# One transfer per expert in place of two, in a two-layer trunk with routed experts

## The chip, the cores and the metric

The kernel runs on one core of a Trainium2 chip. The metric is the device time of one execution in microseconds (us); the median of 3 runs is given. Everything is written in Bass: five instruction streams, one for each engine, that meet only at semaphores.

## What is computed

The reference is a decoder trunk of two layers over 256 tokens of width 1024, all in float32. Layer 0 mixes with a recurrent block, layer 1 with attention over shared keys and values. After its mixer each layer runs a mixture of experts, and that is the part in question:

```python
def moe_ffn(x, router_w, router_b, w_gate, w_up, w_down, s_gate, s_up, s_down):
    ...
    _, e_idx = lax.top_k(choice, TOPK_EXPERTS)          # 8 of 64 experts for each token
    ...
        hdn = jax.nn.silu(xs @ w_gate[e]) * (xs @ w_up[e])
        y = (hdn @ w_down[e]).astype(jnp.float32) * wt[:, None]
        return acc.at[tok].add(y), None
    ...
    shared = (jax.nn.silu(xt @ s_gate) * (xt @ s_up)) @ s_down
    return (acc.astype(x.dtype) + shared).reshape(B, S, D)
```

An expert has w_gate and w_up (1024 x 256 each) and w_down (256 x 1024): 3 x 1 MB of float32. All 64 experts of a layer are used, so each layer reads 192 MB of expert weights.

## The kernel before, in words

**Weights in SBUF.** The tile `weights` holds 18 units of 8 KB per partition. `E(s)` (L202) is expert slot s, three units wide, 24 KB per partition: the first 16 KB (`GU` = 4096 elements) hold gate and up, interleaved by contraction chunk, the last 8 KB hold down. There are four slots, in two pairs: slots 0 and 1 are pair 0, slots 2 and 3 pair 1. In HBM an expert lies in the same layout, 128 rows of 24 KB.

**The expert loop.** Both layers run the same loop, 16 iterations of two pairs (b = 0 and 1), so 64 experts. A pair is two blocks of up to 64 tokens, each in one half of the array's columns. For a pair TensorE does, in this order (L505 to L551): 16 gate/up matmuls 128x512; the scatter of the pair before, in two halves; for b = 1 also the gather of the next iteration's four blocks, by one-hot matmuls; the transposes of the hidden values and of the weighted one-hot; 8 down matmuls 128x512. ScalarE and VectorE evict, scale and split between these.

**What TensorE waits for.** Before a pair's gate/up matmuls it waits for `gu{b}_loaded` (L509), before the down matmuls for `down{b}_loaded` (L541). It counts up `gu_mm` when the gate/up matmuls of a pair are done (L517) and `down_mm` twice, once for each half of the down matmuls (L551).

**What orders the loads.** SyncE's queue issues all weight loads in program order. In `expert_loop` (L287) it reads the numbers of the pair's two experts from a table, waits until the gate/up matmuls of the same pair in the iteration before are done (L295), issues the two gate/up transfers of 2 MB (L297), waits until the down matmuls of that pair are done (L301), and issues the two down transfers of 1 MB (L303). The loop runs for iterations 1 to 15; the experts of iteration 0 are loaded ahead of it by `expert` (L258), again in two transfers each. Transfers of one queue start in the order of issue.

```python
                        sp.wait_ge(S(f"gu_mm_{L}"), i * 2 + (b - 1))
                        ...
                        sp.wait_ge(S(f"down_mm_{L}"), i * 4 + (2 * b - 2))
```

Of the kernel before, what the change touches and what calls it, by code (L numbers as in the profile page):

```python
# [65 lines left out]
EXPERT = 3 * UNIT  # L66
GU = KC * 2 * DE
# [12 lines left out]
def build(nc, xt_d, x_d, pt_d, cst_d, cstb_d, chan_d, rows_d, tab_d, win_d, gates_d, wout_d, shared_d,  # L80
          router_d, experts_d, ple_d, pgate_d, wkv_d, wq_d, wo_d, out_d):
    ctx = ExitStack()
    with ctx:
# [3 lines left out]
        def sem(name):  # L87
            return ctx.enter_context(nc.semaphore(name))
# [100 lines left out]
        def S(name):  # L189
            if name not in names:  # L190
                names[name] = sem(name)
            return names[name]
# [9 lines left out]
        def E(s):  # L202
            return W[:, 3 * s:3 * s + 3, :].rearrange("p a n -> p (a n)")
# [29 lines left out]
        def unit(name):  # L233
            return W[:, loaded_at[name][0], :]
# [18 lines left out]
        @block.sync  # L253
        def _(sp):
            def load(name, src):
                sp.dma_start(unit(name), src).then_inc(unit_sem[loaded_at[name][0]], 16)

            def expert(L, s, e):  # L258
                sp.dma_start(E(s)[:, 0:GU], experts_d[L, e, :, 0:GU]).then_inc(S(f"gu{s // 2}_loaded_{L}"), 16)
                sp.dma_start(E(s)[:, GU:EXPERT], experts_d[L, e, :, GU:EXPERT]).then_inc(S(f"down{s // 2}_loaded_{L}"), 16)  # L260

            sp.dma_start(chan[:, :], chan_d).then_inc(small, 16)
            sp.dma_start(xT[:, :, :], xt_d).then_inc(xt_in, 16)
            for i in range(4):
                load(f"win{i}", win_d[i])
            sp.dma_start(cst[:, :], cst_d).then_inc(small, 16)
            sp.dma_start(bconst[:, :, :], cstb_d).then_inc(small, 16)
            load("gates0", gates_d[0])
            load("gates1", gates_d[1])
            for i in range(4, 8):  # L270
                load(f"win{i}", win_d[i])
            for i in range(4):
                load(f"wout{i}", wout_d[i])
            load("sh0_0", shared_d[0, 0])
            load("sh1_0", shared_d[0, 1])
            sp.wait_ge(S("xb_mm"), KC)
            expert(0, 0, 0)
            sp.wait_ge(S("gate_mm"), KC)
            expert(0, 1, 1)
            for i, u in enumerate(("sh2_0", "pg0_0", "pg1_0", "pg2_0")):  # L280
                sp.wait_ge(S("yb_mm"), 2 * i + 2)
                load(u, shared_d[0, 2] if i == 0 else pgate_d[0, i - 1])
            sp.wait_ge(S("mix_mm"), TC * 2)
            expert(0, 2, 2)
            expert(0, 3, 3)

            def expert_loop(L):  # L287
                sp.wait_ge(S("table"), 1 * L + 1)
                n = sp.value_load(tab[0:1, L, 0, TABLE - 1:TABLE], min_val=NITER_MIN, max_val=NITER_MAX)
                with sp.Fori(1, n) as i:  # L290
                    for b in range(2):
                        es = [sp.value_load(tab[0:1, L, 1, bass.ds(i * 4 + 2 * b + s, 1)], min_val=0, max_val=NE - 1)
                              for s in range(2)]

                        sp.wait_ge(S(f"gu_mm_{L}"), i * 2 + (b - 1))  # L295
                        for s in range(2):
                            sp.dma_start(E(2 * b + s)[:, 0:GU],  # L297
                                         experts_d[L, bass.ds(es[s], 1), :, 0:GU].rearrange("a p n -> (a p) n")
                                         ).then_inc(S(f"gu{b}_loaded_{L}"), 16)

                        sp.wait_ge(S(f"down_mm_{L}"), i * 4 + (2 * b - 2))  # L301
                        for s in range(2):
                            sp.dma_start(E(2 * b + s)[:, GU:EXPERT],  # L303
                                         experts_d[L, bass.ds(es[s], 1), :, GU:EXPERT].rearrange("a p n -> (a p) n")
                                         ).then_inc(S(f"down{b}_loaded_{L}"), 16)
                last = sp.value_load(tab[0:1, L, 0, TABLE - 2:TABLE - 1], min_val=NITER_MIN - 1, max_val=NITER_MAX - 1)
                return n, last

            sp.wait_ge(S("shared_gu_mm"), TC)
            load("pg3_0", pgate_d[0, 3])  # L310
            load("ple_0", ple_d[0])
            sp.wait_ge(S("shared_down_mm"), 1)
            load("wk0", wkv_d[0, 0])
            n, last = expert_loop(0)
            sp.wait_ge(S("down_mm_0"), last * 4 + 2)
            for i in range(1, 4):
                load(f"wk{i}", wkv_d[0, i])
            for i in range(3):
                load(f"wv{i}", wkv_d[1, i])
            sp.wait_ge(S("down_mm_0"), n * 4)  # L320
            load("wv3", wkv_d[1, 3])
            for i in range(4):
                load(f"wq{i}", wq_d[i])
            load("wo0", wo_d[0])
            sp.wait_ge(S("pgate_mm"), TC * 2)
            for i in range(1, 4):
                load(f"wo{i}", wo_d[i])
            load("sh0_1", shared_d[1, 0])
            load("sh1_1", shared_d[1, 1])
            sp.wait_ge(S("k_mm"), TC * 2)  # L330
            load("sh2_1", shared_d[1, 2])
            expert(1, 0, 0)
            sp.wait_ge(S("v_mm"), TC * 2)
            expert(1, 1, 1)
            sp.wait_ge(S("q_mm"), TC * 2)
            expert(1, 2, 2)
            sp.wait_ge(S("mix_mm"), 4 + TC * 2)
            expert(1, 3, 3)
            for i in range(3):
                load(f"pg{i}_1", pgate_d[1, i])  # L340
            sp.wait_ge(S("shared_gu_mm"), 2 + TC)
            load("pg3_1", pgate_d[1, 3])
            load("ple_1", ple_d[1])
            expert_loop(1)
            for c in range(TC):
                for h in range(2):
                    sp.wait_ge(S("x_out"), 4 + 2 * c + h + 1)
                    sp.dma_start(out_d[0, P * c:P * c + P, HALF * h:HALF * h + HALF],
                                 x_res[:, c, HALF * h:HALF * h + HALF]).then_inc(out_s, 16)
            sp.wait_ge(out_s, 16 * TC * 2)  # L350
# [3 lines left out]
        def _(pe):  # L354
# [76 lines left out]
            def moe(L):  # L431
# [72 lines left out]
                n = pe.value_load(tab[0:1, L, 0, TABLE - 1:TABLE], min_val=NITER_MIN, max_val=NITER_MAX)  # L504
                with pe.Fori(0, n) as i:  # L505
                    for b in range(2):
                        g = i * 2 + b

                        pe.wait_ge(S(f"gu{b}_loaded_{L}"), i * 32 + 32)  # L509
                        if b == 0:  # L510
                            pe.wait_ge(S(f"gathered_{L}"), i * 4 + 4)
                        pe.wait_ge(S(f"hidden_{L}"), g + 1)
# [25 lines left out]
                            m = nc.tensor.transpose(PS[:, 7, (2 + c) * P:(3 + c) * P], ohw[:, c, :], ident)  # L538
                        m.then_inc(S(f"turn_mm_{L}"), 1)

                        pe.wait_ge(S(f"down{b}_loaded_{L}"), i * 32 + 32)  # L541
                        pe.wait_ge(S(f"hidT_{L}"), g + 1)
                        if b == 1:
                            pe.wait_ge(S(f"gathered_{L}"), i * 4 + 8)
# [12 lines left out]
            def ple(L):  # L557
# [16 lines left out]
                for t in range(TC * 2):  # L574
# [4 lines left out]
                    m.then_inc(S("pgate_mm"), 1)  # L579

            moe(0)
            ple(0)

# [89 lines left out]
            for c in range(TC):  # L673
                for h in range(2):
                    for k in range(KC):
                        m = mm(bank(2 * c + h), oT[:, k, c * P:c * P + P],
                               kmajor(f"wo{k // 2}")[:, k % 2, h * HALF:h * HALF + HALF], k == 0, k == KC - 1)
                    m.then_inc(S("mix_mm"), 1)
            moe(1)
            ple(1)  # L680

# [609 lines left out]
```

## Time and profile before

| | |
|---|---|
| runs | 1463.49, 1464.17, 1466.36 us; median 1464.17 us |
| profiled execution | 1463.85 us, its span 1462.0 us |
| TensorE busy | 1354.2 us, 93% of the span, 6158 matmuls |
| VectorE, ScalarE, GpSimd busy | 466.7, 291.7, 14.6 us |
| DMA | 460.65 MB, mean 315 GB/s |
| granted TensorE clock, mean | 0.973 |
| expert transfers | 128 of 2048 KB (median 11.1 us from issue to landing), 128 of 1024 KB (8.9 us) |

The span is what the engines take from the first to the last instruction; the execution's own time is 1.85 us longer. A stretch from about 188.5 to 654 us is the expert loop of layer 0, one from about 936.9 to 1406 us that of layer 1. Matmuls are pipelined, so that two of them overlap in the profile and a busy TensorE is not one at its peak. The times below are from the start of the span.

### The profile page before, as it was taken

To read this page: it belongs to the slowest core of one execution; us is meant where nothing else is said; L and a number is where in the kernel's file an instruction comes from. 1 tells how busy PE (TensorE), PEld (TensorE's weight loads), DVE (VectorE), ACT (ScalarE), POOL (GpSimd) and SP (SyncE) were. 2 spreads that over 40 slices of the span, in tenths; PEclk is the share of its full clock that TensorE was granted. 3 is DMA by queue.
4 is the path that set the end of the run, shared out by engine and by line. 5 is a ranking of instruction groups with operands and counts; after the bars stand their busy time and mean duration, and the time that the engine had idled before them with its cause. 6 is when DMAs were issued, how large, how long until landed. Compare 5 with 4: busy or idle time off the path is not lost.

```text
span 1462.0 us, 18637 instructions
## 1 busy us (share of the span) xinstructions
PE 1354.2 (93%) x6158; PEld 687.3 (47%) x6158; DVE 466.7 (32%) x1328; ACT 291.7 (20%) x502; POOL 14.6 (1%) x18
## 2 busy tenths in 40 slices
PE   6976799999999999998799687899999999999988
PEld 5843344544445444543444434454445444454443
DVE  3453433233332333234201324223332333323342
ACT  1502011221112111222201311121112211121121
POOL 0001000000000000000000001000000000000000
PEclk9988999999999999999799897999999999999999
DMA  9924289999999999985322214399999999999900
GB/s 377 387 106 172 87 366 423 423 422 416 417 419 426 420 419 421 422 343 237 144 115 87 87 55 189 153 425 417 414 420 420 420 419 412 419 421 420 404 29 29
DMA packets 46103, 460.65 MB, mean 315 GB/s; under 512 B 5249, under 2 KB 5506, under 8 KB 6658
## 3 DMA queue, kind: packets, MB, share of 16 engines
q1 hardware_dynamic: 44640, 453.48, 74.8%
q10 hardware_dynamic: 1442, 6.88, 1.2%
q8 instruction: 13, 0.21, 0.1%
q14 instruction: 8, 0.07, 0.0%
HBM read 459.30 MB, written 1.05 MB: 315 GB/s over the span
## 4 chain that ended last, share of the span: by engine, by line
PE 81%; DVE 9%; DVEq 4%; ACT 3%; issue 2%; DMA 1%; SPq 0%; ACTq 0%
PE ps L356 77%; DVEq L1095 3%; PE ps L533 1%; DVE onehot L1084 1%; PE ps L538 1%; DVE scratch L931 1%; DVE scratch L1108 1%; ACT y_hi L686 1%; DVE stats L946 1%; DMA weights<-in_win 1%; DVE x_res L963 1%; DVE x_res L968 1%; ACT z L686 1%; ACT scratch L686 1%; PE ps L427 1%
## 5 line engine op out<-in xcount | busy, mean ns | idle before, releaser
L356 PE MATMUL ps<-weights,scratch 128*64 128x512 f32 (+1 forms) x3232 | 749.1, 596 | 11.0 <-DVE scratch L1074 6.9
L356 PEld LDWEIGHTS ps<-weights,scratch 128*64 128x64 f32 (+1 forms) x3232 | 247.2, 140 | 464.2 <-issue 453.9
L686 ACT ACTIVATE scratch<-ps 128x512 f32<-128x512 f32 (+3 forms) x222 | 116.6, 526 | 585.5 <-PE ps L356 578.6
L1124 DVE SCALAR_TENSOR_TENSOR y_lo<-ps,slot_weight,y_hi 128x512 fp32r<-128x512 f32 x128 | 96.1, 750 | 179.8 <-ACT y_hi L686 179.8
L686 ACT ACTIVATE y_hi<-ps,slot_weight 128x512 fp32r<-128x512 f32 x128 | 88.0, 687 | 287.0 <-PE ps L356 287.0
L356 PE MATMUL ps<-weights,xT 128*128 128x512 f32 x320 | 138.5, 593 | 4.5 <-DVE xT L992 3.7
L356 PE MATMUL ps<-onehot,x_hi 128*128 128x256 f32 x544 | 113.5, 290 | 6.1 <-DVE onehot L1084 6.1
L356 PE MATMUL ps<-onehot,x_lo 128*128 128x256 f32 x544 | 110.1, 284 | 0.0
L356 PEld LDWEIGHTS ps<-onehot,x_hi 128*128 128x128 f32 x544 | 86.8, 192 | 35.1 <-issue 32.3
L356 PEld LDWEIGHTS ps<-weights,xT 128*128 128x128 f32 x320 | 60.3, 190 | 78.7 <-issue 74.6
L356 PE MATMUL ps<-y_hi,onehot_T 128*128 128x512 f32 x264 | 91.4, 427 | 3.3 <-DVE y_lo L1124 3.3
L356 PEld LDWEIGHTS ps<-onehot,x_lo 128*128 128x128 f32 x544 | 85.2, 192 | 0.0
L1108 DVE TENSOR_SCALAR scratch<-cst,rankt,wgtt 128x64 f32<-128x64 f32 x256 | 63.0, 309 | 64.4 <-issue 64.3
L356 PE MATMUL ps<-y_lo,onehot_T 128*128 128x512 f32 x264 | 82.7, 394 | 0.0
L1084 DVE TENSOR_SCALAR onehot<-cst,rankt 128x64 fp32r<-128x64 f32 x272 | 49.8, 279 | 88.7 <-issue 78.5
L1116 DVE COPY scratch<-ps 128x256 f32<-128x256 f32 x64 | 27.2, 425 | 155.1 <-PE ps L533 155.1
L1113 DVE TENSOR_TENSOR scratch<-scratch,ps 128x256 f32<-128x256 f32 x64 | 26.7, 417 | 137.3 <-ACT scratch L686 137.3
L356 PE MATMUL ps<-xT,weights 128*128 128x256 f32 x256 | 57.6, 388 | 11.9 <-DMA weights<-in_win 11.9
L356 PEld LDWEIGHTS ps<-xT,weights 128*128 128x128 f32 x256 | 49.8, 195 | 19.0 <-issue 11.9
L356 PEld LDWEIGHTS ps<-y_lo,onehot_T 128*128 128x128 f32 x264 | 49.5, 188 | 11.4
L356 PEld LDWEIGHTS ps<-y_hi,onehot_T 128*128 128x128 f32 x264 | 40.2, 190 | 31.2 <-issue 31.0
L1118 DVE TENSOR_REDUCE slot_weight<-ps 128x1 f32<-128x256 f32 x64 | 27.2, 424 | 46.2 <-PE ps L538 46.2
(139 smaller groups left out, 578.1 us busy)
## 6 DMA issues: line engine op xcount, KB each, us to landing
weights<-in_experts SPq DMA_DIRECT2D x128, 2048.0 KB, 11.1
weights<-in_experts SPq DMA_DIRECT2D x128, 1024.0 KB, 8.9
weights<-in_win SPq DMA_DIRECT2D x8, 1024.0 KB, 20.7
weights<-in_pgate SPq DMA_DIRECT2D x8, 1024.0 KB, 6.0
weights<-in_wkv SPq DMA_DIRECT2D x8, 1024.0 KB, 8.0
weights<-in_shared SPq DMA_DIRECT2D x6, 1024.0 KB, 11.8
weights<-in_wout SPq DMA_DIRECT2D x4, 1024.0 KB, 24.9
lnp<-in_rows ACTq DMA_DIRECT2D x4, 1024.0 KB, 5.3
```

The costliest lines, as they stand in the source:

```text
L356: return nc.tensor.matmul(out, lhsT, rhs, start=first, stop=last, skip_group_check=shared_bank)
L427: m = nc.tensor.transpose(PS[:, 4 + q, (2 * kk + c) * P:(2 * kk + c + 1) * P], src[:, c, k * P:k * P + P], ident)
L533: m = nc.tensor.transpose(PS[:, 6, f * P:f * P + P], hh[:, f * P:f * P + P], ident)
L538: m = nc.tensor.transpose(PS[:, 7, (2 + c) * P:(3 + c) * P], ohw[:, c, :], ident)
L686: return nc.scalar.activation(out, in_, f, **kw)
L1084: ins = v.tensor_scalar(oh[:, c, s * CAP:s * CAP + CAP], iota, rankt[:, c, bass.ds(cols[s], 1)], None, ALU.is_equal)
L1095: return dve.value_load(tab[0:1, L, 0, bass.ds(at, 1)], min_val=0, max_val=NOBLK)
L1108: ins = v.tensor_scalar(ohw[:, c, s * CAP:s * CAP + CAP], iota, rankt[:, c, bass.ds(cols[s], 1)], wgtt[:, c, bass.ds(cols[s], 1)], ALU.is_ ...
L1113: v.tensor_tensor(hh, sg, PS[:, 6, DE:2 * DE], ALU.mult).then_inc(S(f"hidden_{L}"), 1)
L1116: v.tensor_copy(hT.rearrange("p f s -> p (f s)"), PS[:, 6, 0:DE]).then_inc(S(f"hidT_{L}"), 1)
L1118: v.tensor_reduce(wslot[:, 0:1], PS[:, 7, DE:DE + T], AX_X, ALU.max)
L1124: v.scalar_tensor_tensor(y_lo[:, hs], PS[:, 4 + h, :], wslot[:, 0:1], y_hi[:, hs].bitcast(F32), ALU.mult, ALU.subtract).then_inc(S(f"y_out ...
```

## The change

```diff
             def expert(L, s, e):
-                sp.dma_start(E(s)[:, 0:GU], experts_d[L, e, :, 0:GU]).then_inc(S(f"gu{s // 2}_loaded_{L}"), 16)
-                sp.dma_start(E(s)[:, GU:EXPERT], experts_d[L, e, :, GU:EXPERT]).then_inc(S(f"down{s // 2}_loaded_{L}"), 16)
+                sp.dma_start(E(s), experts_d[L, e]).then_inc(S(f"pair{s // 2}_loaded_{L}"), 16)
...
-                        sp.wait_ge(S(f"gu_mm_{L}"), i * 2 + (b - 1))
-                        for s in range(2):
-                            sp.dma_start(E(2 * b + s)[:, 0:GU],
-                                         experts_d[L, bass.ds(es[s], 1), :, 0:GU].rearrange("a p n -> (a p) n")
-                                         ).then_inc(S(f"gu{b}_loaded_{L}"), 16)
-
                         sp.wait_ge(S(f"down_mm_{L}"), i * 4 + (2 * b - 2))
                         for s in range(2):
-                            sp.dma_start(E(2 * b + s)[:, GU:EXPERT],
-                                         experts_d[L, bass.ds(es[s], 1), :, GU:EXPERT].rearrange("a p n -> (a p) n")
-                                         ).then_inc(S(f"down{b}_loaded_{L}"), 16)
+                            sp.dma_start(E(2 * b + s), experts_d[L, bass.ds(es[s], 1)].rearrange("a p n -> (a p) n")
+                                         ).then_inc(S(f"pair{b}_loaded_{L}"), 16)
...
-                        pe.wait_ge(S(f"gu{b}_loaded_{L}"), i * 32 + 32)
+                        pe.wait_ge(S(f"pair{b}_loaded_{L}"), i * 32 + 32)
...
-                        pe.wait_ge(S(f"down{b}_loaded_{L}"), i * 32 + 32)
```

An expert comes in one transfer of 3 MB, 24 KB per partition. Both transfers of a pair are issued when the pair's down matmuls of the iteration before are done; the wait on the gate/up matmuls is gone. TensorE waits for the whole pair ahead of the gate/up matmuls and for nothing loaded ahead of the down matmuls.

On SyncE, in the body of the expert loop of layer 0, this stands for pair 0 before (L297 are the gate/up transfers, 128x4096; L303 the down transfers, 128x2048):

```order
L295 ISA
L297 ISA [waits gu_mm_0]
L297 DMA weights<-in_experts 128x4096
L297 ISA
L297 DMA weights<-in_experts 128x4096
L301 REGISTER_ALU
L303 ISA [waits down_mm_0]
L303 DMA weights<-in_experts 128x2048
L303 ISA
L303 DMA weights<-in_experts 128x2048
```

and this in the changed kernel:

```order
L294 REGISTER_ALU
L296 ISA [waits down_mm_0]
L296 DMA weights<-in_experts 128x6144
L296 ISA
L296 DMA weights<-in_experts 128x6144
```

The gate/up part has moved behind the wait on the down matmuls and is one transfer with the down part.

On TensorE, around the change from pair 0 to pair 1 in the same loop, this stands before (98 and 99 of its list are the down matmuls of pair 0, then come the gate/up matmuls of pair 1):

```order
L538 MATMUL ps<-cst,scratch 128x128 [waits weighted_0]
L538 MATMUL ps<-cst,scratch 128x128
L356 MATMUL ps<-weights,scratch 64x512 [waits hidT_0,down0_loaded_0]
L356 MATMUL ps<-weights,scratch 64x512 x7
L356 MATMUL ps<-weights,scratch 64x512 [waits hidden_0,gu1_loaded_0]
L356 MATMUL ps<-weights,scratch 64x512 x15
```

and this in the changed kernel (its L348 is L356 of before):

```order
L530 MATMUL ps<-cst,scratch 128x128 [waits weighted_0]
L530 MATMUL ps<-cst,scratch 128x128
L348 MATMUL ps<-weights,scratch 64x512 [waits hidT_0]
L348 MATMUL ps<-weights,scratch 64x512 x7
L348 MATMUL ps<-weights,scratch 64x512 [waits hidden_0,pair1_loaded_0]
L348 MATMUL ps<-weights,scratch 64x512 x15
```

No matmul has moved; the wait for the down part is gone, and the wait ahead of the gate/up matmuls now stands for both parts.

## Rows read from the trace of the kernel before

**Rows 1.** The page: busy time by engine, and the chain that ended last.

```profile
PE 1354.2 (93%) x6158; PEld 687.3 (47%) x6158; DVE 466.7 (32%) x1328; ACT 291.7 (20%) x502; POOL 14.6 (1%) x18
...
PE 81%; DVE 9%; DVEq 4%; ACT 3%; issue 2%; DMA 1%; SPq 0%; ACTq 0%
```

**Rows 2.** Busy time of both expert loops; last: clock, DMA share, GB/s.

```profile
188.50:654.00 465.50, 465.40 (x2373) 222.92 (x2372) 146.11 (x430) 92.81 (x157) 0.00 (x0) 1.00 0.99 415
936.90:1406.00 469.10, 466.46 (x2378) 223.63 (x2377) 146.53 (x431) 92.80 (x157) 0.00 (x0) 1.00 0.96 402
```

**Rows 3.** Waits of SyncE's queue: us in total, times, longest.

```profile
SPq L303 <- PE ps L356: 421.6, 60, 8.9
SPq L297 <- PE ps L356: 278.8, 60, 14.1
```

**Rows 4.** Timeline of SyncE, one iteration of layer 0 (start, us, what).

```profile
431.72 0.85 SPq L303 DMA_DIRECT2D weights<-in_experts  x2
438.62 0.96 SPq L297 DMA_DIRECT2D weights<-in_experts  x2
448.48 0.85 SPq L303 DMA_DIRECT2D weights<-in_experts  x2
455.33 0.86 SPq L297 DMA_DIRECT2D weights<-in_experts  x2
461.62 0.85 SPq L303 DMA_DIRECT2D weights<-in_experts  x2
```

**Rows 5.** Timeline of SyncE, first iteration of layer 1.

```profile
941.82 0.85 SPq L303 DMA_DIRECT2D weights<-in_experts  x2
...
958.58 0.85 SPq L303 DMA_DIRECT2D weights<-in_experts  x2
...
971.98 0.85 SPq L303 DMA_DIRECT2D weights<-in_experts  x2
```

**Rows 6.** DMA issues: the transfers issued at 455.33, 455.86, 461.62, us to landing.

```profile
weights<-in_experts SPq DMA_DIRECT2D x1, 2048.0 KB, 9.7
...
weights<-in_experts SPq DMA_DIRECT2D x1, 2048.0 KB, 14.1
...
weights<-in_experts SPq DMA_DIRECT2D x1, 1024.0 KB, 10.4
```

**Rows 7.** SyncE's issues of experts 2 and 3 of layer 0.

```profile
122.67 0.33 SPq L259 DMA_DIRECT2D weights<-in_experts  x1
...
124.00 0.62 SPq L260 DMA_DIRECT2D weights<-in_experts  x1
```

**Rows 8.** DMA issues: landing of the last, issued at 124.00 us.

```profile
weights<-in_experts SPq DMA_DIRECT2D x1, 1024.0 KB, 16.3
```

**Rows 9.** SyncE at 935.72 us, and the landings of the two transfers.

```profile
935.72 0.88 SPq L297 DMA_DIRECT2D weights<-in_experts  x2
...
weights<-in_experts SPq DMA_DIRECT2D x1, 2048.0 KB, 7.5
...
weights<-in_experts SPq DMA_DIRECT2D x1, 2048.0 KB, 11.8
```

**Rows 10.** SyncE at 186.19 us, and the landing of the second transfer.

```profile
186.19 0.87 SPq L297 DMA_DIRECT2D weights<-in_experts  x2
...
weights<-in_experts SPq DMA_DIRECT2D x1, 2048.0 KB, 12.8
```

**Rows 11.** TensorE timeline; in brackets its idle time before.

```profile
143.41 13.90 PE L356 MATMUL ps<-weights,xT 128*128 128x512 f32 x32
...
162.11 8.83 PE L356 MATMUL ps<-weights,scratch 128*128 128x512 f32 x16 [3.43 <-DVE scratch L1074]
...
174.09 0.48 PE L356 MATMUL ps<-onehot,x_hi 128*128 128x256 f32 x2 [3.00 <-DVE onehot L1084]
...
910.16 8.66 PE L356 MATMUL ps<-weights,scratch 128*128 128x512 f32 x16 [3.44 <-DVE scratch L1074]
```

**Rows 12.** TensorE by microsecond: busy (matmuls), granted clock, DMA.

```profile
162.00:163.00 1.00, 0.89 (x2) 0.67 1.01 418
163.00:164.00 1.00, 1.00 (x3) 0.50 0.94 385
...
166.00:167.00 1.00, 1.00 (x4) 1.00 0.00 0
...
172.00:173.00 1.00, 0.00 (x0) 1.00 0.46 115
...
174.00:175.00 1.00, 0.92 (x8) 1.00 1.00 426
```

## The prediction

> **What bounds the kernel now.** I read the page first: TensorE is busy for 93% of the span and is 81% of the chain that ended last [rows 1]. Then busy time by stage. In the expert loops TensorE has next to no idle time, 0.1 us in 465.5 and 2.6 us in 469.1, at full clock, and the DMA engines are busy for 0.99 and 0.96 of the same stretches at 415 and 402 GB/s [rows 2]. Two resources are full at once. Which of them paces? The queue that issues the loads answers it: SyncE always waits for TensorE, 421.6 us ahead of the down transfers and 278.8 us ahead of the gate/up transfers, 60 times each [rows 3], so 2 layers x 15 iterations x 2 pairs. TensorE paces the loop, and the loads keep up with little to spare. Whatever makes them later shows.
>
> The issue times give the period. The down matmuls of the pairs end at 431.72, 448.48 and 461.62 [rows 4]: pair 1 takes 16.76 us from the end of pair 0, pair 0 takes 13.14 us from the end of pair 1, the period is 29.90 us. In layer 1 the same ends are 941.82, 958.58 and 971.98 [rows 5]: 16.76 and 13.40 us.
>
> **The change, part by part.** An iteration must bring 4 x 3.146 MB = 12.58 MB, before and after. What moves is the time of issue. Before, the gate/up part of pair 1 (4.19 MB of 6.29) was issued at 438.62 and TensorE wanted it at 461.62, 23.0 us later. Now all of it is issued at 448.48, with 13.14 us to go.
>
> How long does a pair take to land? No row shows two transfers of 3 MB, so I bound it. The nearest is the first load of experts 2 and 3, 6.29 MB in four transfers into an idle queue: issued from 122.67, the last one issued at 124.00 and landed 16.3 us later, at 140.30 [rows 7, 8], which is 17.6 us. From the start of layer 1's loop, 4.19 MB issued at 935.72 landed at 943.2 and, the second transfer being issued 0.55 us after the first, at 948.1 [rows 9]: 12.4 us for both, and 4.85 us for each further 2.10 MB (432 GB/s), so 17.2 us for three times 2.10 MB. The same at the start of layer 0's loop: 186.73 + 12.8 = 199.5, which is 13.3 us after the issue [rows 10], plus 4.85 is 18.2, the high end. For the low end: the same bytes in four transfers took 17.6 and in three would take 17.2, so two might save another 0.4: 16.8. I take 17.2, from rows 9, since there the loop's own instructions start on an idle queue. With 0.1 for the hand-over (my choice, small beside the bounds), TensorE can start a pair 17.3 us after the issue.
>
> *Pair 1 waits.* Its loads are issued at the end of its down matmuls; pair 0 then needs 13.14 us (layer 0) or 13.40 (layer 1). The rest is idle time of TensorE: 17.3 - 13.14 = 4.16 us and 17.3 - 13.40 = 3.90 us, in each of 15 iterations. 15 x (4.16 + 3.90) = 120.9 us. Nothing hides it: the scatter and the gather that could fill it stand behind the gate/up matmuls in TensorE's program, and in the loop before TensorE had no idle time that could swallow it [rows 2].
>
> *Pair 0 does not.* Its loads are issued when its own down matmuls end; before it is needed again pair 1 waits 4.1 us and works 16.76, so 20.9 us. Its data queue behind the tail of pair 1's. Transfers of the queue land in order: those issued at 455.33 and 455.86 landed at 465.0 and 470.0, the next, issued at 461.62, at 472.0 [rows 4, 6]. Behind the earlier pair, which lands 4.1 us after this issue, pair 0 lands 14.6 us later (three times 4.85), at 18.7: 2.2 us in hand. And the queue is idle when pair 1's loads are issued, so that these start as in rows 9. Only in the first looped iteration, with no stall ahead, does pair 0 wait 17.3 - 16.8 = 0.5 us, once in each layer: 1.0 us.
>
> *The clock.* A TensorE that idles for 4 us each period may lose its clock. Two idle stretches of 3.43 and 3.44 us stand in the trace; the same number of matmuls after them took 8.83 and 8.66 us where half of 13.90 is 6.95 [rows 11], a loss of 1.9 and 1.7. The granted clock was at 0.50 in 163:164, from the first microsecond after the gap, and back at 1.00 by 166; after the 3.00 us without a matmul ahead of 174.09 [rows 11] it stayed at 1.00 [rows 12]. Stalls of 3.9 to 4.2 us are longer than all three. A longer gap lets part of the half-clock time fall into the gap itself, where it costs nothing, so I take 1.5 us for each stall, with ends of 1.0 and 1.9 (the low one a guess, were half the time to fall into the gap): 30 x 1.5 = 45 us. It falls into pair 1, which is TensorE's work throughout, so it lengthens the period in full.
>
> *What is removed.* 120 issues and two waits per pair on SyncE, one wait on TensorE: nothing waited for them, as SyncE sat waiting for TensorE before each [rows 3]. In the loads ahead of the loop, experts 2 and 3 of layer 0 landed at 140.3, before the shared expert's matmuls even start [rows 8, 11]; merged or not, they are early. Zero. The loads behind the loop are issued relative to its end and shift with it. Zero.
>
> **The sum.** 1463.85 (the profiled execution's own time, 0.3 below the median of the runs) + 120.9 + 1.0 + 45 = 1630.8 us; against the median 1631.1. I predict 1631.
>
> One formula would come out lower. The Trainium skill, "DMA: Bandwidth & Descriptors", section "Anatomy of one DMA", gives a fixed 2.0 us plus the bytes over 436 GB/s for a DMA; an estimate from that page for a pair is 2.0 + 14.4 = 16.4 us, stalls of 3.4 and 3.1 us, and 1606 us in all. It was fitted on another way of issuing, and rows 7 to 9 measure the thing itself on this queue, so they decide.
>
> **The rivals.**
>
> *The clock stays up.* For: the gap of 3.0 us left it up. Against: both gaps of 3.4 us did not, and these are longer. Without the 45 us: 1586. If only some of the stalls cost it, between 1586 and 1631.
>
> *The loads of the two pairs share the engines.* Pair 0's loads are issued about 4 us before pair 1's have landed, with some 3 us of data left. If they took turns, pair 1 would land 3 us later: 30 x 3 = 90 more, 1721. Against: landings in order, 2 us apart for the next 1.05 MB [rows 6].
>
> *Faster.* The loop could be paced by its DMAs, not by TensorE: they are 0.99 busy at only 415 GB/s, while two transfers in a row land at 432. If long rows of 24 KB brought that rate throughout, 12.58 MB would take 29.1 us in place of 29.9, 30 x 0.8 = 24 us less: 1440. It decides only if a pair lands within 13.14 us of its issue, else the stall comes first; with no fixed cost at all that is 479 GB/s. Against: 432 measured, and TensorE's waits show no DMA in the loop. The Trainium skill speaks for this side too: "DMA: Bandwidth & Descriptors", section "Rules for kernel authors", advises to coalesce many small transfers into one large and to move at least 1 MiB at a time; by it alone the change could only help. No row here shows a transfer below 1 MB that is held back.
>
> *No difference.* If TensorE's program let the stall be filled, nothing would be lost; the order of its instructions rules this out, and there is no spare time in the loop either [rows 2].
>
> **How the numbers follow.** My forecast has 0.86 (the stall of pair 1 with the clock loss), the clock that stays up 0.07, sharing loads 0.05, faster 0.01, no difference 0.01. A measurement of this kernel tells about 0.2% (3 us) from no change. The forecast's own bounds are 16.8 us and 1.0 us: 1463.85 + 15 x (3.76 + 3.50) + 30 + 0.2 = 1603; and 18.2 and 1.9: 1463.85 + 15 x (5.16 + 4.90) + 57 + 3 = 1675. Both at their worst together is unlikely, so the top is 1660; the bottom reaches down to 1595, toward the case in which only some stalls cost the clock. Slower by over 0.2% is 0.98.
>
> **What would show it.** Right: TensorE's waits of 3.7 to 4.5 us at the gate/up matmuls, released by the load of weights, in pair 1 only, 30 of them, some 121 us in total; a period of 35.6 us in the loop (17.3 + 16.8 + 1.5); a granted clock of 0.50 for a few microseconds in each period; DMA idle for several microseconds in each period, landings of 16 to 18 us for the second transfer of a pair. The stages outside the loops keep their lengths. Wrong: stalls ahead of pair 0 as well, or stalls of 7 us (sharing); a clock of 1.00 throughout (1586); a period of 30 us.

## The result, and the profile after

| | before | changed |
|---|---|---|
| median | 1465.04 us (4 runs, 1463.49 to 1466.36) | 1681.35 us (4 runs, 1679.03 to 1683.09) |
| ratio | | 1.1476 (95% interval 1.1454 to 1.1497) |
| profiled execution, its span | 1463.85, 1462.0 us | 1683.09, 1681.2 us |
| mean granted TensorE clock | 0.973 | 0.919 |

The change costs 15%. The direction and the place were as predicted, the size was not: 216 us where 166 were forecast, and 1681 lies outside the range (1595 to 1660).

The page of the changed kernel, against [rows 1]:

```profile
PE 1444.2 (86%) x6158; PEld 703.5 (42%) x6158; DVE 467.0 (28%) x1328; ACT 291.5 (17%) x502; POOL 14.5 (1%) x18
...
PE 59%; DMA 31%; DVE 6%; ACT 2%; issue 1%; SPq 1%; DVEq 0%; ACTq 0%
PE ps L348 57%; DMA weights<-in_experts 30%; SPq L296 1%; DVE scratch L922 1%; DVE stats L937 1%; DMA weights<-in_win 1%; DVE x_res L954 1%; DVE x_res L959 1%; ACT z L677 1%; PE ps L419 1%; ACT scratch L677 1%; DVE z L964 0%; PE ps L525 0%; PE ps L530 0%; PE ps L641 0%
```

The loads of experts were nowhere in the chain that ended last; now they are 30% of it. VectorE, ScalarE and GpSimd do the same work in the same time. TensorE runs the same 6158 matmuls and is busy 90 us longer. (The counts are records of the trace; the expert matmuls have two each, so that a pair's 16 gate/up matmuls stand as x32.)

The waits of the changed kernel (us in total, times, longest):

```profile
PE ps L348 <- DMA weights<-in_experts: 131.3, 32, 4.8
```

and the expert matmuls, grouped by form, of the kernel before and, second, of the changed one (busy us, mean ns of one | idle before):

```profile
L356 PE MATMUL ps<-weights,scratch 128*64 128x512 f32 x3072 | 673.8, 594 | 1.5 <-ACT scratch L686 1.5
```

```profile
L348 PE MATMUL ps<-weights,scratch 128*64 128x512 f32 x3072 | 760.8, 652 | 132.8 <-DMA weights<-in_experts 131.3 <-ACT scratch L677 1.5
```

Two numbers hold the whole result: 131.3 us of idle time that a load ends, and 760.8 - 673.8 = 87.0 us more for the same matmuls, 218.3 together; the profiled executions differ by 219.2. The 32 waits are 15 ahead of pair 1 in each layer and one ahead of pair 0 in each layer's first looped iteration. Of the 30 ahead of pair 1, 29 are followed by slow gate/up matmuls. TensorE's timeline around three of them (start, us, what, idle time before):

```profile
228.32 8.78 PE L348 MATMUL ps<-weights,scratch 128*64 128x512 f32 x32 [3.29 <-DMA weights<-in_experts]
...
452.04 10.00 PE L348 MATMUL ps<-weights,scratch 128*64 128x512 f32 x32 [4.55 <-DMA weights<-in_experts]
...
1090.79 7.09 PE L348 MATMUL ps<-weights,scratch 128*64 128x512 f32 x32 [2.78 <-DMA weights<-in_experts]
```

At full clock they take 7.09 us. After 2.78 us of idle time they still do, after 3.29 they lose 1.7, after 4.55 they lose 2.9. Of the 30 stalls of pair 1, 26 are of the last kind (2.5 to 3.0 us lost). By microsecond around the middle one (after the length: TensorE busy, then weight loads, VectorE, ScalarE and GpSimd; the last three columns are granted clock, DMA share, GB/s):

```profile
450.00:451.00 1.00, 0.00 (x0) 0.00 (x0) 0.79 (x4) 0.00 (x0) 0.00 (x0) 1.00 0.97 418
451.00:452.00 1.00, 0.00 (x0) 0.00 (x0) 0.00 (x0) 0.00 (x0) 0.00 (x0) 0.56 0.97 418
452.00:453.00 1.00, 0.96 (x4) 0.35 (x6) 0.00 (x0) 0.00 (x0) 0.00 (x0) 0.50 1.03 442
...
457.00:458.00 1.00, 1.00 (x4) 0.24 (x2) 0.00 (x0) 0.00 (x0) 0.00 (x0) 0.53 1.20 516
458.00:459.00 1.00, 1.00 (x8) 0.41 (x6) 0.00 (x0) 0.00 (x0) 0.00 (x0) 1.00 1.03 442
```

The clock falls to half at about 451.1, 0.9 us ahead of the first matmul, and is back at about 457.9: 6.8 us at half, of which 5.9 are worked. The length of the gap alone does not set this. After a stall of 4.20 us in layer 1 the clock fell only at about 1386.4, 1.0 us into the matmuls (columns: TensorE busy, clock, DMA share, GB/s):

```profile
1385.36 8.78 PE L348 MATMUL ps<-weights,scratch 128*64 128x512 f32 x32 [4.20 <-DMA weights<-in_experts]
```

```profile
1385.00:1386.00 1.00, 0.64 (x4) 1.00 0.91 393
1386.00:1387.00 1.00, 1.00 (x5) 0.69 1.03 442
...
1389.00:1390.00 1.00, 1.00 (x4) 0.61 0.97 418
```

There it was at half for 3.4 us, all of them worked, and 1.7 us were lost. In the 26 stalls that cost 2.5 us or more it fell 0.7 to 1.7 us ahead of the first matmul and stayed at half for 6.8 us.

The chain of waits shows one stall from end to end:

```profile
430.74 3.61 PE ps L348 x16
434.35 0.02 issue
...
434.51 0.33 SPq L296
...
435.04 16.96 DMA weights<-in_experts
451.99 0.04 issue
452.04 14.94 PE ps L348 x68
```

Down matmuls, issue, 17.0 us of loading, next matmuls. From the first issue at 434.51 to the landing at 451.99 are 17.5 us, against 13.14 us of other work. The period is 37.6 us (434.51 to 472.11) where it was 29.90 [rows 4].

### The profile page after: what moved, and what is told of

It is laid out like the page before. It is cut to its first block, busy times and chain, and to the rows that moved or that the text cites. A ratio compares the mean times of both kernels' runs of the same rounds, so it can differ in the third digit from the quotient of the medians.

```text
span 1681.2 us, 18175 instructions
## 1 busy us (share of the span) xinstructions
PE 1444.2 (86%) x6158; PEld 703.5 (42%) x6158; DVE 467.0 (28%) x1328; ACT 291.5 (17%) x502; POOL 14.5 (1%) x18
## 4 chain that ended last, share of the span: by engine, by line
PE 59%; DMA 31%; DVE 6%; ACT 2%; issue 1%; SPq 1%; DVEq 0%; ACTq 0%
PE ps L348 57%; DMA weights<-in_experts 30%; SPq L296 1%; DVE scratch L922 1%; DVE stats L937 1%; DMA weights<-in_win 1%; DVE x_res L954 1%; DVE x_res L959 1%; ACT z L677 1%; PE ps L419 1%; ACT scratch L677 1%; DVE z L964 0%; PE ps L525 0%; PE ps L530 0%; PE ps L641 0%
## 5 line engine op out<-in xcount | busy, mean ns | idle before, releaser
L348 PE MATMUL ps<-weights,scratch 128*64 128x512 f32 (+1 forms) x3232 | 836.3, 651 | 142.3 <-DMA weights<-in_experts 131.3
L348 PEld LDWEIGHTS ps<-weights,scratch 128*64 128x64 f32 (+1 forms) x3232 | 261.9, 152 | 668.0 <-issue 503.0
L348 PE MATMUL ps<-weights,xT 128*128 128x512 f32 x320 | 138.5, 593 | 4.5 <-DVE xT L983 3.7
L348 PE MATMUL ps<-onehot,x_hi 128*128 128x256 f32 x544 | 113.5, 291 | 6.0 <-DVE onehot L1075 6.0
L348 PE MATMUL ps<-onehot,x_lo 128*128 128x256 f32 x544 | 110.1, 284 | 0.0
L348 PEld LDWEIGHTS ps<-onehot,x_hi 128*128 128x128 f32 x544 | 86.7, 192 | 34.9 <-issue 32.2
L348 PE MATMUL ps<-y_hi,onehot_T 128*128 128x512 f32 x264 | 91.5, 428 | 3.3 <-DVE y_lo L1115 3.3
L348 PEld LDWEIGHTS ps<-weights,xT 128*128 128x128 f32 x320 | 60.4, 190 | 78.6 <-issue 74.5
L348 PEld LDWEIGHTS ps<-onehot,x_lo 128*128 128x128 f32 x544 | 85.3, 193 | 0.0
L348 PE MATMUL ps<-y_lo,onehot_T 128*128 128x512 f32 x264 | 82.6, 394 | 0.0
L348 PE MATMUL ps<-xT,weights 128*128 128x256 f32 x256 | 58.6, 392 | 12.0 <-DMA weights<-in_win 12.0
L348 PEld LDWEIGHTS ps<-xT,weights 128*128 128x128 f32 x256 | 50.5, 198 | 19.3 <-issue 12.0
L348 PEld LDWEIGHTS ps<-y_lo,onehot_T 128*128 128x128 f32 x264 | 49.6, 188 | 11.4
L348 PEld LDWEIGHTS ps<-y_hi,onehot_T 128*128 128x128 f32 x264 | 40.2, 190 | 31.2 <-issue 31.0
```

What stands on the lines that cost most here:

```text
L348: return nc.tensor.matmul(out, lhsT, rhs, start=first, stop=last, skip_group_check=shared_bank)
```

## The experiments

Each was timed beside the kernel before on the same chip.

**1. The late issue alone.** The kernel before with all four transfers and both waits, but everything issued behind the wait on the down matmuls:

```diff
-                        sp.wait_ge(S(f"gu_mm_{L}"), i * 2 + (b - 1))
+                        sp.wait_ge(S(f"down_mm_{L}"), i * 4 + (2 * b - 2))
                         for s in range(2):
                             sp.dma_start(E(2 * b + s)[:, 0:GU],
...
-                        sp.wait_ge(S(f"down_mm_{L}"), i * 4 + (2 * b - 2))
                         for s in range(2):
                             sp.dma_start(E(2 * b + s)[:, GU:EXPERT],
...
```

> The kernel before with its four transfers and its two waits, but all four issued when the pair's down matmuls are done: the late issue alone, without the merging. Theory A (the loss comes from TensorE having to wait for all 6.29 MB ahead of the gate/up matmuls): the gate/up part, 4.19 MB, lands some 12.4 us after the issue, and TensorE has 13.14 to 13.40 us, so there is no stall or one of under 0.5 us, and the clock stays up: 1464 to 1475 us. Rival B (the late issue by itself starves the loop, since the DMA engines were full before): 1600 us or more.

Measured: 1464.96 us, ratio 0.9997 (0.9986 to 1.0007), 11 runs. TensorE's waits for experts:

```profile
  PEld ps L355: 12.2, 30
  PE ps L355: 0.2, 1
```

No stall but one of 0.2 us. The weight loads wait 0.4 us each, which the array hides. So the late issue by itself costs nothing, although the gate/up parts are issued 6.3 us (pair 0) and 9.9 us (pair 1) later than in [rows 4]. Theory A held, rival B fell.

**2. One wait, four transfers.** The changed kernel with each expert cut into 2 MB and 1 MB again, both on the pair's semaphore:

```diff
-                            sp.dma_start(E(2 * b + s), experts_d[L, bass.ds(es[s], 1)].rearrange("a p n -> (a p) n")
+                            sp.dma_start(E(2 * b + s)[:, 0:GU],
+                                         experts_d[L, bass.ds(es[s], 1), :, 0:GU].rearrange("a p n -> (a p) n")
+                                         ).then_inc(S(f"pair{b}_loaded_{L}"), 16)
+                            sp.dma_start(E(2 * b + s)[:, GU:EXPERT],
+                                         experts_d[L, bass.ds(es[s], 1), :, GU:EXPERT].rearrange("a p n -> (a p) n")
                                          ).then_inc(S(f"pair{b}_loaded_{L}"), 16)
...
-                        pe.wait_ge(S(f"pair{b}_loaded_{L}"), i * 32 + 32)
+                        pe.wait_ge(S(f"pair{b}_loaded_{L}"), i * 64 + 64)
```

> The changed kernel with each expert's transfer cut into two again (2 MB and 1 MB, one behind the other), both counted by the same semaphore: late issue and one wait for the pair, without the merging. Theory A: the merging itself neither costs nor gains; the pair lands within 0.4 us of the changed kernel's, 1678 to 1695 us. Rival B (rows of 24 KB make the transfer slow): back toward 1600 us, stalls below 4 us.

Measured: 1676.93 us, ratio 1.1454 (1.1436 to 1.1471). Its expert matmuls:

```profile
L353 PE MATMUL ps<-weights,scratch 128*64 128x512 f32 x3072 | 756.6, 649 | 130.1 <-DMA weights<-in_experts 128.5 <-ACT scratch L682 1.5
```

128.5 us of stalls and 82.8 us of slow matmuls, against 131.3 and 87.0. The time is 1 us below the expected range. The transfer of 3 MB is no better than its two parts; the 4.4 us by which it is slower are hardly clear of the noise (the intervals of the ratios overlap), and 2.4 of the 2.8 us between the stalls are one stall, the first of pair 1 in layer 1 (0.41 us in place of 2.78). Theory A held: given the late issue, the merging costs only because the gate/up matmuls then wait for the down weights too.

Run 1 shows that the late issue without the merged wait is free. The merged wait without the late issue was not run. In the kernel before the last down transfer of pair 1 is this one (SyncE's timeline; us to landing):

```profile
449.00 0.33 SPq L303 DMA_DIRECT2D weights<-in_experts  x1
...
weights<-in_experts SPq DMA_DIRECT2D x1, 1024.0 KB, 11.1
```

It landed at 460.1, and pair 1's gate/up matmuls began at about 461.4. An estimate from these rows is that a merged wait with the early issue would have found both parts there. The loss then takes both halves of the change, and one transfer for each expert brings both, since the buffer of its down part comes free last.

**3. Keeping the array busy through the stall.** The changed kernel with n matmuls of unused result ahead of pair 1's wait; bank 6 is free there:

```diff
+                        if b == 1:
+                            for _ in range(n):
+                                mm(PS[:, 6, :], ident, x_res[:, 0, 0:HALF], True, True, True)
                         pe.wait_ge(S(f"pair{b}_loaded_{L}"), i * 32 + 32)
```

With n = 10:

> The changed kernel with ten matmuls of 128x512 whose result is not used, ahead of pair 1's wait for its load: some 4.3 us of work in the stall. Theory A (of the loss, 131 us are stalls and 87 us are gate/up matmuls at half clock, 2.9 us each): the clock stays at 1.00, the stall stays as it is, and the 87 us go: 1683 - 87 = 1596, plus some 4 us in each of the two first iterations that have no stall, so 1598 to 1612 us. Rival B (the longer gate/up matmuls come from reading weights while the DMA engines write others, not from the clock): no gain, 1683 us or more.

Measured: 1751.06 us, ratio 1.1958 (1.1940 to 1.1976), so neither number. I had taken 0.43 us for one full-width matmul, which is what one of a pair on column halves takes (7.09 us for 16). Its rows (x640 are 320 matmuls):

```profile
L348 PE MATMUL ps<-weights,scratch 128*64 128x512 f32 x3072 | 680.8, 595 | 1.5 <-ACT scratch L680 1.5
L348 PE MATMUL ps<-x_res,cst 128*128 128x512 f32 x640 | 283.2, 597 | 0.0
```

Ten take 8.85 us (283.2 / 32), twice the stall; no wait for a load is left, and the expert matmuls are back at 680.8 us. The clock theory had that part right; the time needed the right n. So n = 5, 3, 2 and 1:

> The changed kernel with five of the matmuls of unused result ahead of pair 1's wait, not ten: one takes 0.88 us (8.85 us for ten in the run before), so ten were 4.4 us longer than the stall that they should fill, and five, 4.4 us, fill it. Theory A (the gate/up matmuls after a stall are slow by the clock alone): the clock stays at 1.00 in the loop, the gate/up matmuls take 7.1 us again in place of 10.0, the 87 us go, and the two first iterations, which have no stall, pay 4.4 us each: 1681 - 87 + 9 = 1603, 1598 to 1610 us. Rival B (they are slow by contention with the loads): 1681 us or more.

> The same with three: 2.6 us of work and 1.7 us idle in each stall. Theory A (the clock is lost by idle time of over 3 us, not by any): clock at 1.00, 1681 - 87 + 5 = 1599 us. Rival B (any gap costs a part in proportion to its length): about 1632 us.

> The same with two: 1.8 us of work and 2.6 us idle. Theory A: as with three, 1597 to 1600 us, since a gap of 3.0 us left the clock alone in the kernel before. Rival B (in proportion): about 1648 us.

> The same with one: 0.9 us of work and 3.5 us idle, as long as the gaps of the kernel before that cost 1.7 and 1.9 us. Theory A with my price of before (1.5 to 1.9 us a stall): 1681 - 87 + 2 + 30 x 1.7 = 1647 us, clock at half for some 3.3 us after each. If the price of the changed kernel holds for this gap too (2.9 us, half clock for over 6 us): 1683 us.

| n | idle before gate/up, in total | expert matmuls busy | mean clock | time |
|---|---|---|---|---|
| 0 (changed kernel) | 131.3 us | 760.8 us | 0.919 | 1681.35 us |
| 1 | 101.0 | 763.3 | 0.918 | 1686.96, ratio 1.1522 (1.1499 to 1.1545) |
| 2 | 75.4 | 698.0 | 0.968 | 1622.47, ratio 1.1082 (1.1055 to 1.1108) |
| 3 | 48.9 | 684.2 | 0.983 | 1607.64, ratio 1.0980 (1.0956 to 1.1005) |
| 5 | 0.6 | 680.8 | 0.978 | 1614.51, ratio 1.1021 (1.0994 to 1.1047) |

The rows with n = 2 and n = 1 show single stalls. n = 2:

```profile
264.90 8.78 PE L348 MATMUL ps<-weights,scratch 128*64 128x512 f32 x32 [3.04 <-DMA weights<-in_experts]
...
301.10 7.09 PE L348 MATMUL ps<-weights,scratch 128*64 128x512 f32 x32 [2.44 <-DMA weights<-in_experts]
```

n = 1:

```profile
265.24 9.97 PE L348 MATMUL ps<-weights,scratch 128*64 128x512 f32 x32 [3.53 <-DMA weights<-in_experts]
```

The stall itself, work and idle time together, stays; what the filling buys is the clock. From n = 0 to 3 the time falls by 73.7 us and the matmuls' busy time by 76.6. Contention with the loads is ruled out: the loads run on as before while the matmuls are back at 680.8. One set of gate/up matmuls of pair 1 with n = 5 and, second, of the changed kernel (columns as above):

```profile
613.60:620.70 7.10, 7.10 (x33) 2.29 (x33) 0.00 (x0) 0.00 (x0) 0.00 (x0) 1.00 1.02 440
```

```profile
452.00:462.00 10.00, 9.96 (x33) 2.87 (x33) 0.00 (x0) 0.00 (x0) 0.00 (x0) 0.70 1.01 435
```

The same loads at 440 and 435 GB/s stand beside both. The 7 us that are left above the 673.8 of the kernel before come without any loss of clock (they stand with n = 5 and 10 too), some 0.2 us for each of the 32 breaks in a stream of expert matmuls whose records otherwise overlap; so of the 87.0 us of the changed kernel 80.0 are the clock's.

All four times came out above Theory A's: 1614.5 against 1598 to 1610, 1607.6 against 1599, 1622.5 against 1597 to 1600, 1687.0 against 1647 (1683 by the price of the changed kernel). The breaks were in none of the sums, and with n = 2 ten of the 30 stalls still cost 1.7 us each (698.0 - 680.8 = 17.2). Nor is the loss in proportion to the gap (1632 and 1648 were expected by that rival; 1608 and 1622 came): it is 0.1 us for each stall with n = 3 (1.6 us idle on average), 0.6 with n = 2 (2.5 us) and 2.75 with n = 1 (3.3 us). My price of 1.7 us for a gap of 3.5 (1647 us) fell with n = 1, where 27 stalls had 6.8 us at half clock. With n = 5 the median is 7 us above n = 3, about 5 us between runs of the same mean clock: the five take 4.56 us, a little more than the stall, and are paid in full where there is no stall.

**4. Real work in the stall.** The first two gathers of pair 1 moved from behind the gate/up matmuls to ahead of the wait for the load:

```diff
+                        if b == 1:
+                            pe.wait_ge(S(f"y_out_{L}"), g * 2 + 2)
+                            pe.wait_ge(S(f"onehot_{L}"), i + 2)
+                            gather(0, 4)
+                            gather(1, 5)
                         pe.wait_ge(S(f"pair{b}_loaded_{L}"), i * 32 + 32)
...
-                        pe.wait_ge(S(f"y_out_{L}"), g * 2 + 2)
-                        if b == 1:
-                            pe.wait_ge(S(f"onehot_{L}"), i + 2)
-                            gather(0, 4)
-                            gather(1, 5)
+                        if b == 0:
+                            pe.wait_ge(S(f"y_out_{L}"), g * 2 + 2)
```

> The changed kernel with the first two gathers of pair 1 (16 matmul pairs of 128x256, 1.9 us) put ahead of pair 1's wait for its load instead of behind its gate/up matmuls. Theory A: 1.9 us of each stall are filled with work that was on the path, 30 x 1.9 = 57 us; what stays idle falls into two parts of some 1.6 us (waiting for y_out) and under 1 us, after which the clock stays at 1.00, another 87 us: 1683 - 57 - 87 = 1539, 1530 to 1550 us. Rival B (the clock falls all the same): 1626 us.

Measured: 1553.29 us, ratio 1.0607 (1.0591 to 1.0623); 3 us above the range given, on Theory A's side. (The two gathers are 16 matmuls, not 16 pairs.) Its waits:

```profile
PE ps L348 <- DVE y_lo L1117: 56.1, 34, 1.7
...
PE ps L348 <- DMA weights<-in_experts: 18.4, 30, 1.1
```

The stall is split in two, 1.65 us until VectorE has emptied the banks and 0.6 us for the load, with 2.2 us of work between (390.91 to 393.08 in one of them, where I had expected 1.9); the expert matmuls take 680.8 us and the mean clock is 0.982. This order gives back 128 us of the 216 and still leaves 88.

**5. Which matmuls come after the stall.** The same move, but behind the wait, so that the stall stays whole and full-width matmuls follow it (the diff is that of 4 with the new lines behind the wait for the load):

> The changed kernel with the first two gathers of pair 1 between the wait for its load and its gate/up matmuls: the same work, the stall as long as before (4.4 us), but the first matmuls after it are full-width ones (128x256 on 128 columns, 1.9 us at full clock) and not those on halves of the columns. Theory A (the half clock lasts 6.2 to 6.8 us because the fall comes ahead of the first matmul, whatever that is): as the changed kernel, 2.9 us for each stall, 1678 to 1688 us. Rival B (the matmuls on column halves are what holds the clock down; full-width ones brought it back after some 3.3 us in the kernel before): 1.7 us for each stall, 1681 - 36 = 1645 us.

Measured: 1693.53 us, ratio 1.1566 (1.1533 to 1.1600). One stall in its timeline, and the clock at its start and end:

```profile
418.64 0.79 PE L348 MATMUL ps<-onehot,x_hi 128*128 128x256 f32 x2 [4.77 <-DMA weights<-in_experts]
...
422.34 7.83 PE L348 MATMUL ps<-weights,scratch 128*64 128x512 f32 x32
```

```profile
417.00:418.00 1.00, 0.00 (x0) 0.53 1.15 492
418.00:419.00 1.00, 0.36 (x1) 0.50 1.03 442
...
423.00:424.00 1.00, 1.00 (x4) 0.56 0.91 393
```

From about 417.1 to 423.9, again 6.8 us at half clock. The gathers and the expert matmuls together are 87.5 us slower than before (145.4 + 137.0 + 702.5 busy, against 113.5 + 110.1 + 673.8), the same 87. Rival B fell: the kind of matmul doesn't matter. The time is 5.5 us above the expected range and 12 above the changed kernel; 7.5 us of that are longer stalls, 138.8 us in total in place of 131.3. Why they are longer was not tried.

**6. Fewer bytes.** The changed kernel without the down part of slot 3 in the loop's loads:

```diff
+                            n_el = GU if 2 * b + s == 3 else EXPERT
-                            sp.dma_start(E(2 * b + s), experts_d[L, bass.ds(es[s], 1)].rearrange("a p n -> (a p) n")
+                            sp.dma_start(E(2 * b + s)[:, 0:n_el],
+                                         experts_d[L, bass.ds(es[s], 1), :, 0:n_el].rearrange("a p n -> (a p) n")
```

> The changed kernel with the down part of slot 3 left out of the loop's loads (1 MB of the 6 MB of pair 1; its down matmuls then use the weights of iteration 0). Theory A (the stall is the landing of the pair's bytes less 13.1 to 13.4 us, and the clock cost goes when the stall is under some 2.5 us): the pair lands 1.05 MB earlier, 2.4 us at 432 GB/s, the stalls fall from 4.38 to 1.96 us on average, the clock stays: 1681 - 73 - 87 = 1521 us, 1512 to 1530. Rival B (the stall is set by when the queue is free or by a fixed latency, not by the bytes): stalls above 3.5 us, 1650 us or more.

Measured: 1542.66 us, ratio 1.0536 (1.0470 to 1.0602). Its timeline at two stalls of pair 1 and one of pair 0:

```profile
387.18 7.09 PE L350 MATMUL ps<-weights,scratch 128*64 128x512 f32 x32 [2.15 <-DMA weights<-in_experts]
405.49 4.94 PE L350 MATMUL ps<-weights,scratch 128*64 128x512 f32 x22 [1.33 <-DMA weights<-in_experts]
...
583.86 8.78 PE L350 MATMUL ps<-weights,scratch 128*64 128x512 f32 x32 [2.09 <-DMA weights<-in_experts]
```

Most stalls of pair 1 are at about 2 us, as the bytes have it (4.3 less 2.4), and rival B fell. With shorter stalls pair 0 has less time, and its loads come late now and then (405.49: 1.33 us), after which pair 1's own stall is shorter; all waits together are 60.5 us at 39 places, only 2 more than the 58 in the expectation. What put the time 22 us above it is the matmuls: 698.2 us busy where 673.8 were expected, 7 of them the breaks and 17 the clock. It is not safe at 2 us: of two stalls of 2.15 and 2.09 us one left it alone and one cost 1.7 us. My limit of 2.5 us was too sharp.

## Why the prediction was right in kind and wrong in size

*What bounds the kernel.* Right: TensorE paced the loop. Run 1 shows that the slack of the loads was larger than I said ("the loads keep up with little to spare"; "whatever makes them later shows"): all of them could be issued up to 10 us later at no cost, as long as TensorE waited for each part where it needs it. A DMA share of 0.99 was a full queue, not a late one.

*Pair 1 waits.* Right. 30 stalls of 4.06 to 4.80 us but for the first of each layer (3.29 and 2.78), where 4.16 and 3.90 were forecast. The pair landed 17.5 us after its issue, not 17.2 (from the first issue to the first matmul 17.2 to 17.8 us in the 30 stalls). Off by 9.4 us in all (131.3 against 121.9).

*Pair 0 does not.* Right for the changed kernel, but its one wait per layer was 1.24 and 1.88 us, not 0.5.

*The clock.* This is the step that failed: "so I take 1.5 us for each stall, with ends of 1.0 and 1.9". It was about 2.9 us in 26 of the 30 stalls and 80.0 / 30 = 2.7 on average, and with the 7 us of stopping and starting, which I had no term for, 87 us in place of 45, beyond my upper end of 57. I had argued that with a longer gap part of the half-clock time falls into the gap, where it costs nothing. A part does: the fall comes 0.7 to 1.7 us ahead of the first matmul. But the half clock then lasts 6.8 us and not the 3.4 that the two gaps of the kernel before had, so that more of it is worked, not less: (6.8 - 0.9) / 2 = 2.95 us for the middle stall shown above. A row against my price stood in the kernel before, and I passed it over: after its idle time of 9.39 us, which ends at 92.42, the clock was

```profile
92.00:93.00 1.00, 0.57 (x1) 0.50 0.00 0
...
97.00:98.00 1.00, 1.00 (x3) 0.75 0.42 168
98.00:99.00 1.00, 1.00 (x4) 1.00 0.05 20
```

at half until about 97.5, 5.1 us into the work, a cost of some 2.5 us. I priced stalls of 4.2 us from the two gaps that were shorter and left out the next longer one. With its 2.5 as the upper end my bounds would have been 1603 to 1693 (1463.85 + 150.9 + 75 + 3), and 1681 lies within them; but I had also cut 1675 down to 1660 for the range.

*The rivals.* The clock that stays up is ruled out by the rows, loads that share the engines by stalls of 4.3 us and not 7, faster and no difference by the result. The sum with the measured terms: 1463.85 + 131.3 + 87.0 = 1682.2, measured 1683.1. The estimate by the formula of the Trainium skill, "DMA: Bandwidth & Descriptors", section "Anatomy of one DMA" (16.4 us for a pair), is 1.1 us below the 17.5 that were measured; the rows of the trace were the better source [rows 7 to 10]. The same page of the Trainium skill, section "Rules for kernel authors", asks for at least 1 MiB in each DMA, which both kernels meet, and so gives no reason to go on to 3 MB; that by it the change could only help was my reading. Run 2 shows 2 MB and 1 MB transfers at least as fast as 3 MB ones.

## What to carry to other kernels

Merging two transfers also merges what the consumer waits for. Ask of each part when it is first needed and when its buffer comes free: here the down weights are needed 9 us after the gate/up weights (pair 0's matmuls begin at 457.9 and 448.5 us in the trace before), and the merged wait threw that away. The late issue by itself was free; together with the merged wait it was not. And price a stall of TensorE with the clock that follows it, by the longest gap in the trace as well as by those nearest in length; here a stall cost two thirds of its own length again (87.0 against 131.3 us).

## What the runs showed of the hardware that I had not expected

- In the changed kernel the granted clock was at half for 6.8 us in 26 of the 30 stalls of pair 1 (4.06 to 4.80 us idle) and for 3.4 us in three (3.29, 4.16 and 4.20 us); in run 5 it was 6.8 us in 28 of 30, so that full-width matmuls after the stall did not differ from column-half ones. Where it fell after the first matmul had begun, it was at half for 3.4 us every time (two stalls here, all ten that lost any with n = 2); where it fell 0.7 us or more ahead of it, for 6.8 us in 26 of 27. What decides when it falls was not tested.
- After 2.78 and 2.44 us it stayed at 1.00; stalls of 2.09 and 3.04 us cost 1.7 us, one of 2.15 nothing. So the length of the gap alone doesn't set the cost.
- In layer 0 the period was 37.5 us on average in the changed kernel (264.80 to 752.36), with n = 1 (265.24 to 602.88) and in run 5 (268.43 to 756.33), although the stalls have 4.5, 3.4 and 4.7 us of idle time. Why was not tested.
- Each pair of 3 MB transfers of pair 1 landed about 17.5 us after its issue, on a queue that had been idle (DMA share 0.00 from 428 to 434.5). With two transfers for each expert the stalls, but for the first of each layer, were 4.32 us on average against 4.36.
